# Out product, norms and turning in one block, the root's split last, and six edits to the attention, SSM and HGRN stages

## The reference, cut to what matters

```python
def first_block(x, ...):
    h = rms_norm(x, attn_pre_norm)
    h = dilated_attention_mixer(h, w_in, w_out, rel_bias)    # (o * silu(z)) @ w_out
    x = x + rms_norm(h, attn_post_norm)
    h = rms_norm(x, ssm_pre_norm)
    h = s5_mixer(h, ...)                                     # (y * silu(z)) @ w_out
    x = x + rms_norm(h, ssm_post_norm)
    return x

def s5_scan(u, a_re, a_im, log_dt, b, c, d_skip):            # 64 groups of 16 channels, 64 states
    a_bar = jnp.exp(A * dt)
    b_bar = ((a_bar - 1.0) / A)[..., None] * Bm
    states = associative_scan(combine, (a_bar, u @ b_bar))
    y = real(states @ C) + d_skip * u

def hgrn2(h, ...):                                           # 8 heads
    f = lb + (1.0 - lb) * sigmoid(f); logf = log(f); kin = 1.0 - f
    G = cumsum(logf); o = (q * exp(G)) @ state + tril(q, k, decay) @ v
    o = rms_norm_2(o, gnorm) * silu(g); return o @ w_out
```

## Time and profile before

| | us |
|---|---|
| median of 3 runs | 4160.52 |
| lowest, highest | 4149.19, 4170.95 |
| the profiled execution, its time | 4150.93 |
| its span | 4149.1 |
| TensorE busy | 3700.0 (89%) |
| VectorE busy | 1690.6 (41%) |
| ScalarE busy | 894.7 (22%) |
| GpSimd busy | 1896.0 (46%) |

### The profile page before, as it was taken

The page is one execution under the profiler, slowest core; times in us unless marked ns, Lnnn a source line. Parts: engine busy times, 40 slices in busy tenths (PEclk is TensorE's granted clock), DMA queues, the critical chain, the costliest instruction groups (busy, mean ns, idle before and its releaser), DMA issues. The chain is left out here.

```text
span 4149.1 us, 47884 instructions
## 1 busy us (share of the span) xinstructions
PE 3700.0 (89%) x18444; PEld 3021.7 (73%) x18444; DVE 1690.6 (41%) x2738; ACT 894.7 (22%) x2343; POOL 1896.0 (46%) x731
## 2 busy tenths in 40 slices
PE   8998987399788799999966899997899999879999
PEld 6777864278676588877855788875788877768887
DVE  2323137877536531132367411245521144652213
ACT  2333241111213410011033111013211112331111
POOL 5444431221343255655634465652356554335564
PEclk9999996687799799999988999998999999989999
DMA  3327851033222122222200222221222222212222
GB/s 135 103 92 93 109 79 42 25 92 92 67 88 73 68 83 97 96 92 90 97 21 1 77 102 101 91 102 51 77 92 92 101 85 90 72 69 89 101 91 81
DMA packets 95957, 342.06 MB, mean 82 GB/s; under 512 B 27078, under 2 KB 45766, under 8 KB 61208
## 3 DMA queue, kind: packets, MB, share of 16 engines
q1 hardware_dynamic: 83408, 314.22, 25.4%
q10 hardware_dynamic: 12360, 25.18, 1.8%
HBM read 318.39 MB, written 16.78 MB: 81 GB/s over the span
## 5 line engine op out<-in xcount | busy, mean ns | idle before, releaser
L294 POOL CAST wh<-raw 128x2048 fp32r<-128x2048 f32 x269 | 513.7, 1910 | 1778.3 <-PE bank L336 1424.2
L296 POOL TENSOR_TENSOR wl<-raw,wh 128x2048 fp32r<-128x2048 f32 x269 | 1243.6, 4623 | 21.5
L334 PE MATMUL bank<-XTh,wh 128*128 128x512 f32 (+1 forms) x2448 | 953.1, 389 | 45.0 <-DVE XTl L1028 15.0
L335 PE MATMUL bank<-XTh,wl 128*128 128x512 f32 (+1 forms) x2448 | 937.2, 383 | 0.0
L336 PE MATMUL bank<-XTl,wh 128*128 128x512 f32 (+1 forms) x2448 | 936.4, 383 | 0.0
L334 PEld LDWEIGHTS bank<-XTh,wh 128*128 128x128 f32 x2448 | 468.7, 191 | 155.4 <-issue 42.5
L336 PEld LDWEIGHTS bank<-XTl,wh 128*128 128x128 f32 x2448 | 467.4, 191 | 90.3
L335 PEld LDWEIGHTS bank<-XTh,wl 128*128 128x128 f32 x2448 | 469.0, 192 | 84.7
L334 PE MATMUL bank<-wh,XTh 128*128 128x512 f32 (+2 forms) x1056 | 393.0, 372 | 36.8 <-DVE XTl L1028 12.6
L335 PE MATMUL bank<-wh,HTl 128*128 128x512 f32 x1024 | 403.4, 394 | 0.0
L334 PE MATMUL bank<-wh,HTh 128*128 128x512 f32 x1024 | 401.7, 392 | 0.0
(11 more groups left out here) (343 smaller groups left out, 4233.7 us busy)
## 6 DMA issues: line engine op xcount, KB each, us to landing
raw<-in_weights SPq DMA_DIRECT2D x270, 1024.0 KB, 4.8
B<-bias_d ACTq DMA_DIRECT2D x8, 1024.0 KB, 5.6
B<-bias_a ACTq DMA_DIRECT2D x8, 512.0 KB, 10.7
bias_d<-O SPq DMA_DIRECT2D x16, 256.0 KB, 18.8
MO<-HS SPq DMA_DIRECT2D x64, 64.0 KB, 2.6
bc<-in_ln_g ACTq DMA_DIRECT2D x8, 512.0 KB, 6.7
bc<-in_ln_b ACTq DMA_DIRECT2D x8, 512.0 KB, 7.1
X<-in_x SPq DMA_DIRECT2D x4, 512.0 KB, 9.0
```

Source lines behind the costliest of these rows:

```text
L294: pool.tensor_copy(wh[s][:, :], raw[r][:, :]).then_inc(w_high.h, 1)
L296: pool.tensor_tensor(wl[s][:, :], raw[r][:, :], wh[s][:, :].bitcast(F32), ALU.subtract).then_inc(w_split.h, 1)
L334: nc.tensor.matmul(psum, sh, mh, start=first, stop=False)
L335: nc.tensor.matmul(psum, sl, mh, start=False, stop=False)
```

## The change

1. `out_phase` is one block, with the norms and the turning in it. VectorE no longer copies the banks: `weigh` multiplies them by the norm's vector into `Y`, and ScalarE squares out of PSUM. The roots, the addition, the second norm (where there is one, its gain is now a row vector and no longer applied after the turning) and the turning go token tile by token tile. Half 1 of the product is done in the order `LATE`. GpSimd splits three of the four weight chunks ahead of the first root and the last, the next stage's first, behind the last root.
2. The table of phases leaves `arithmetic`. It is now `phases`, called in `ssm_scan` on VectorE behind `add_skip(0)`, ahead of `prepare(1)`; a squaring takes 4 instructions instead of 6, and there are 8. The three pole tables have a semaphore of their own. SP waits for `phases` before one of its transfers, since the scratch `T` lies in memory that the transfer writes.
3. `outputs` interleaves the two groups of a pair.
4. The passes of the dilated attention are written out on TensorE.
5. In the sliding attention the projection comes behind `scores(j+3)`.
6. HGRN: the logarithms and scans stand before the token tiles (`G` lies in `Y`, which makes room); in `hgrn_heads` `W` has eight slots, squares have a buffer of their own and come at n = 3, and the root at n = 6.

```diff
-def out_phase(vec, transposed, scalars=None):
+tail = {k: signal("tail_" + k) for k in ("vectors", "sums", "root", "x_new", "x_sums", "x_root", "normed", "turned", "high", "low")}
+LATE = ((0, 0), (1, 0), (2, 0), (0, 1), (3, 0), (1, 1), (2, 1), (3, 1))
+def out_phase(vec, gain=None, scalars=None):
...
-        out_product(bc, [vec], squares, scalars)
-        norm_phase("rms_add", bc=bc, transposed=transposed)
-def out_product(bc, vecs, squares, scalars):
...
+        def split(first, n):
+            a = c0 + AHEAD + first
+            stream(pool, a, a + n, 2, lambda k, j: split_chunk(pool, k, j % RAW, j % SPLIT))
...
+        def root(tt):
+            r = st[:, tt:tt + 1]
+            pool.wait_ge(*at("sums", TT + tt + 1))
+            link(p.tensor_tensor(r, SQ[:, 0, tt:tt + 1], SQ[:, 1, tt:tt + 1], ALU.add))
+            link(p.tensor_scalar(r, r, 1.0, RMS_EPS, ALU.mult, ALU.add))
+            power(r, tail["root"])
...
+        split(0, 3)
+        root(0)
+        root(1)
+        x_root(0)
+        root(2)
+        x_root(1)
+        root(3)
+        x_root(2)
+        x_root(3)
+        split(3, 1)
+        link.done()
...
+        def turn(tt):
+            pe.wait_ge(*at("normed" if second else "x_new", tt + 1))
+            for half in range(2):
+                for k in range(4):
+                    r = nc.tensor.transpose(bank(half, tt)[:, P * k:P * k + P],
+                                            src[:, tt, 512 * half + P * k:512 * half + P * k + P], ident[:, :])
+                r.then_inc(tail["turned"].h, 1)
+        for kh in range(2):
+            for tt in range(TT):
+                out_tile(0, tt, kh)
+        for tt, kh in LATE:
+            out_tile(1, tt, kh)
...
+        def square(half, tt):
+            if tt == TT - 1:
+                act.wait_ge(w_used.h, CREDIT + c0 + 2 * half + 2)
+            else:
+                act.wait_ge(tile_done.h, pe_done + 3 * half + tt + 1)
+            a.activation(N[:, tt, cols(half)], bank(half, tt), ACT.Square, scale=D ** -0.5,
+                         accum_out=SQ[:, half, tt:tt + 1]).then_inc(tail["sums"].h, 1)
+        def x_square(tt):
+            if second:
+                act.wait_ge(*at("x_new", tt + 1))
+                a.activation(N[:, tt, :], X[:, tt, :], ACT.Square, scale=D ** -0.5,
+                             accum_out=st[:, TT + tt:TT + tt + 1]).then_inc(tail["x_sums"].h, 1)
...
+            square(0, tt)
+        square(1, 0)
+        square(1, 1)
+        x_square(0)
+        square(1, 2)
+        x_square(1)
+        square(1, 3)
+        x_square(2)
+        if not second:
+            high(0)
+        x_square(3)
+        for tt in range(second ^ 1, TT):
+            high(tt)
...
+        def weigh(half, tt):
+            dve.wait_ge(*at("sums", TT * half + tt + 1))
+            link(v.tensor_tensor(Y[:, tt, cols(half)], bank(half, tt), bc[0][:, cols(half)], ALU.mult))
+        def add(tt):
+            dve.wait_ge(*at("root", tt + 1))
+            v.scalar_tensor_tensor(X[:, tt, :], Y[:, tt, :], st[:, tt:tt + 1], X[:, tt, :], ALU.mult, ALU.add).then_inc(tail["x_new"].h, 1)
+        def norm(tt):
+            if second:
+                dve.wait_ge(*at("x_root", tt + 1))
+                v.scalar_tensor_tensor(N[:, tt, :], X[:, tt, :], st[:, TT + tt:TT + tt + 1], bc[1][:, :],
+                                       ALU.mult, ALU.mult).then_inc(tail["normed"].h, 1)
+        def low(tt):
+            for half in range(2):
+                dve.wait_ge(*at("high", 2 * tt + half + 1))
+                v.tensor_tensor(tokens(XTl, half, tt), blocks(bank(half, tt)), tokens(XTh, half, tt).bitcast(F32),
+                                ALU.subtract).then_inc(tail["low"].h, 1)
+        for tt in range(TT):
+            weigh(0, tt)
+        weigh(1, 0)
+        add(0)
+        weigh(1, 1)
+        add(1)
+        norm(0)
+        weigh(1, 2)
+        add(2)
+        norm(1)
+        weigh(1, 3)
+        add(3)
+        low(0)
+        norm(2)
+        low(1)
+        norm(3)
+        low(2)
+        low(3)
...
-            with pe.Fori(0, PASSES - 1) as i:
-                one_pass(i, False)
-            one_pass(PASSES - 1, True)
+            for i in range(PASSES):
+                one_pass(i, i == PASSES - 1)
...
         def fill(j, d):
-            if d == 0 and tile_at(j) is not None:
+            if d == (j >= 0) and tile_at(j) is not None:
                 project(tile_at(j))
...
     with ExitStack() as c:
-        G = sb("G", [P, TT, D], F32, c)
+        G = Y
         with ExitStack() as c2:
...
                     a.activation(SG[:, n % 2, :], PS[n % 4][:, :], ACT.Sigmoid).then_inc(a_b.h, 1)
+                for h in range(8):
+                    act.wait_ge(tile_free.h, tile_free.base + 9 + h)
+                    a.activation(LF[:, h, :], LF[:, h, :], ACT.Ln).then_inc(a_b.h, 1)
                 for n in range(8, 16):
                     wait_g(act, n)
                     a.activation(G[:, n % 4, 512 * (n // 4 - 2):512 * (n // 4 - 1)], PS[4 + n % 4][:, :], ACT.Sigmoid).then_inc(a_b.h, 1)
-                act.wait_ge(tile2_free.h, tile2_free.base + 16)
-                for h in range(8):
-                    a.activation(LF[:, h, :], LF[:, h, :], ACT.Ln).then_inc(a_b.h, 1)
...
                         v.tensor_scalar(KIN[:, h, :], LF[:, h, :], -1.0, 1.0, ALU.mult, ALU.add).then_inc(tile_free.h, 1)
+                for h in range(8):
+                    dve.wait_ge(a_b.h, a_b.base + 18 + h)
+                    v.tensor_tensor_scan(LF[:, h, :], ones[:, :], LF[:, h, :], 0.0, ALU.mult, ALU.add)
...
-                for h in range(8):
-                    dve.wait_ge(a_b.h, a_b.base + 26 + h)
-                    v.tensor_tensor_scan(LF[:, h, :], ones[:, :], LF[:, h, :], 0.0, ALU.mult, ALU.add)
...
+    SLOTS = 8
-        W = sb("W", [P, 4, S], F32, c)
+        W = sb("W", [P, SLOTS, S], F32, c)
+        squared = sb("squared", [P, 2, S], F32, c)
...
-        def w(b, n):
-            return W[:, (SL * b + n) % 4, :]
+        def w(h, n):
+            return W[:, (SL * h + n) % SLOTS, :]
...
-                    if n == 5 and 2 * i + b:
+                    if n == 6 and 2 * i + b:
...
+            if h >= 2:
+                act.wait_ge(head["sums"].h, head["sums"].base + 4 * (h - 1))
-                a.activation(Y[:, cc, P * h:P * h + P], PS[6 + b][:, P * cc:P * cc + P], ACT.Square,
+                a.activation(squared[:, b, P * cc:P * cc + P], PS[6 + b][:, P * cc:P * cc + P], ACT.Square,
...
-            sp.dma_start(d, t[x]).then_inc(sm["params"].h, 16)
+            sp.dma_start(d, t[x]).then_inc(sm["poles" if x in ("ssm_a_re", "ssm_a_im", "ssm_log_dt") else "params"].h, 16)
+        act.wait_ge(sm["poles"].h, 16 * 3)
...
+        dve.wait_ge(sm["params"].h, 16 * 6)
...
+    def phases(self, dve, link):
+        v, T, E = nc.vector, self.T, self.tab.E
+        mul, cmul = complex_ops(dve, link)
+        s = lambda k: self.s[:, k, :]
-        t2 = (s(14), s(15))
+        t1, t2 = s(14), s(15)
+        def square(o, x):
+            mul(t1, x[0], x[0])
+            mul(t2, x[1], x[1])
+            link(v.tensor_tensor(o[0], t1, t2, ALU.subtract))
+            link(v.scalar_tensor_tensor(o[1], x[0], 2.0, x[1], ALU.mult, ALU.mult))
-            cmul(nxt, cur, cur, *t2)
+            square(nxt, cur)
...
+            sp.wait_ge(*at("phases", 1))
...
-        for g in range(2 * QP):
-            lo, pr = 64 * (g % 2), g // 2
-            o = PS[6 + g % 2][:, 256 * (k % 2) + 64 * pr:256 * (k % 2) + 64 * pr + 64]
-            nc.tensor.matmul(o, MO[:, k % 2, pr, g % 2, :], U[:, 8 * k + g, :], start=True, stop=False)
+        place = lambda pr, g: PS[6 + g][:, 256 * (k % 2) + 64 * pr:256 * (k % 2) + 64 * pr + 64]
+        for pr in range(QP):
+            for g in range(2):
+                nc.tensor.matmul(place(pr, g), MO[:, k % 2, pr, g, :], U[:, 8 * k + 2 * pr + g, :], start=True, stop=False)
-                r = nc.tensor.matmul(o, CA[lo:lo + 64, k % 3, x, pr, 1:9, :].rearrange("p n c -> p (n c)"),
-                                     SPR[lo:lo + 64, x, pr, :], start=False, stop=x == 1)
+                for g in range(2):
+                    lo = 64 * g
+                    r = nc.tensor.matmul(place(pr, g), CA[lo:lo + 64, k % 3, x, pr, 1:9, :].rearrange("p n c -> p (n c)"),
+                                         SPR[lo:lo + 64, x, pr, :], start=False, stop=x == 1)
...
+        if not k:
+            scalars.phases(dve, link)
+            dve.sem_inc(sm["phases"].h, 1)
...
-    with ExitStack() as c:
-        out_phase(t["attn_post_norm"][0], False, SsmScalars(ssm_tables, c))
-    ssm_mixer(ssm_tables)
-out_phase(t["ssm_post_norm"][0], "layer0" in STAGES)
+    ssm_scalars = SsmScalars(ssm_tables, s_scope)
+    out_phase(t["attn_post_norm"][0], t["ssm_pre_norm"][0], ssm_scalars)
+    ssm_mixer(ssm_tables, ssm_scalars)
+out_phase(t["ssm_post_norm"][0])
```

(3 more changed lines are left out.)

150 lines of the change are left out of this document (89 added, 61 removed).

## The result

| | before | after |
|---|---|---|
| median of 4 runs, us | 4154.85 | 4037.57 |
| lowest, highest | 4148.5, 4170.95 | 4028.74, 4051.03 |
| profiled execution | 4150.93 | 4051.03 |
| its span | 4149.1 | 4049.2 |

The ratio is 0.9715, 95% interval 0.9674 to 0.9756: 101 to 135 us less. Forecast were 4063 and a range of 4029 to 4098. The two profiled executions differ by 99.9 us, where the prediction's sum had 92.6. The profiled execution of after is the slowest of its four.

The account below looks back on a forecast made before the run. TensorE, busy 89% of 4149.1 us, was taken as the bound: only its idle or repeated time can be won. Terms sum to -92.6, from 4150.9 to 4058.3; half of 9.6 added gives 4063, range 4029 to 4098.

Parts of the forecast that it names:

- Written-out passes: Dilated attention: TensorE's two gaps at the loop's returns, 2.91 and 11.02 us, both vanish, -13.9 us.
- First tail: Norms between the first two layers: 70.8 us from last product to next shrink to 20.5, -50.3 us.
- The table: Table of phases moved into the SSM scan: all of it on the path, with shorter squarings, +27.2 us.
- Outputs in pairs: SSM scan's outputs: CA products of two groups overlap in row halves, -11 us, bounds -4 and -25.
- Second tail: The stretch from T = 1165.3 to 1185.16: 19.8 us shrink to 10.4, -9.4 us (-4 to -12).
- Heads: HGRN's heads: eight slots let ScalarE run ahead; a quarter of VectorE's 31.9 us wait goes, -8 us.
- Sliding attention: Projection behind the scores: three quarters of TensorE's 22.6 us of waits for probabilities go, -17 us.
- (d): Rival: written-out passes in dilated attention stall on instruction fetches, slower, up to 4220 us; chance 0.03.
- (a): Rival: some overlaps in outputs, heads and sliding attention do not come, 22 us less gain, 4085; chance 0.2.
- (b): Rival: more is hidden: outputs -20, heads -20, tail 16 instead of 20.5, so 4037 us; chance 0.12.
- (c): Rival: the gaps of TensorE's loop stay, 13.9 us less gain, 4077 us; chance 0.07.
- (e): Rival: no change that can be told, 70 us of terms failing together; chance 0.03.

Follow-up runs that it names:

- the inverse edit: The loop of TensorE's passes in the dilated attention put back into the changed kernel: median 4066.58 us of 4 runs.

## Why the prediction was right

The measured 4037.57 lies in the range, 25.4 below the forecast. The profiled executions' difference of 99.9 was 7.3 more than the sum of 92.6. The prediction then added 4.7 because the median before lay above its profiled execution. After, the median lies 13.5 below its profiled one, so this term had the wrong sign; 7.3, 4.7 and 13.5 are the 25.4. Of the mechanism all but the heads held. Point by point:

- **Written-out passes, -13.9: mis-sized, -17.2.** The gaps were right; the low clock behind each of them, 1.6 and 1.9 us, was left out, though a stretch just behind them would have shown it.
- **First tail, -50.3: -50.8.** The queue of low parts behind `high(0)` was there, and so was the split's hold. That the sum came within 0.5 is in part luck: the hold was 3.9 for the 2.5 charged, `norm(2)` stood in the queue as well, and the low parts of tile 2, which were charged, came behind the last norm, beside its turning.
- **The table, +27.2: +27.1.** All of it was on the path, nothing of it was hidden, and the eight squarings were sized right. That it would have cost as much in the old place, so that moving it gains nothing, was not said.
- **Outputs in pairs, -11: about -14.7.** The last two outputs gave 10.2, of which the gate's longer low clock took back 1.6: 8.6 for the 8.5 forecast. (The 10.2 already has in it 1.2 lost to the new wait for `MO`.) The steady steps gave 6.1 for 2.5, and their term was mis-sized twice over: a step's outputs save 4.9 of TensorE, not 2.4, and they save nothing where VectorE is held but all of it in the step without a split.
- **Second tail, -9.4: -9.4.** The split held the last addition, 2.82 instead of 1.28, 1.5 for the 1.0 charged.
- **Scans, -10.2: -9.0**, and 8.9 when undone. TensorE's wait itself fell by exactly the 10.2, from 14.68 to 4.48.
- **Heads, -8: -5.7, and the reason was wrong.** The step that failed is "Eight slots let ScalarE run ahead": four slots are as fast. The cause of the gain stays open.
- **Sliding attention, -17: -19.6.** More of the waits went than three quarters of 22.6.
- **The working.** Three numbers of it don't come out and change nothing in the sum. The product's last three tiles end 2.7 us apart and not 4.7, since a record of 0.39 starts 0.23 behind the one before it. All of the outputs on the path would be 8.5 + 14.4 = 23 and not 25. And rival (d) would decide from eight stalls on (78.7 / 11.02), while the range by its own working is 4026 to 4096.
- **Rivals.** (a) fell with the outputs and the sliding attention. (b) is the nearest: its 4037 is the median that came, but not by its parts; the tail was not 16, the heads gave no 20, and the outputs gave 14.7 of its 20. (c), that the gaps stay, is refuted by the inverse edit; the 0.3 us that a branch and a compare-and-branch of the Trainium skill ("Advanced Engine Details and Errata", Control Flow Timing) would give is not what a return costs here, 2.88 and 10.36. (d), slower by fetching in a row, is refuted: 131 packets, and no stall that the loop hadn't. That sequential code hides its fetches and a far branch doesn't, as the Trainium skill has it ("Runtime: NRT & Kernel Launch", Instruction fetch mechanics), these runs agree with. (e), no change that can be told, fell with the measured 101 to 135.

## What to carry to other kernels

A stage that moves work from one wait to another shows a large gain in the place where it was and the same loss in the place where it is; add both before calling it a gain, as with the 27 us of the table. Where two engines wait for each other in turn by equal amounts in every step, look for an order that only the program text imposes; taking `prepare` a step ahead gave 33 us of the scan. Where work is taken off an engine and a wait of the same length appears, as TensorE's 4.8 did behind the paired outputs, a second chain is as long, and the gain comes only when that one is shortened too. And a wait that changes its name without changing its length, as VectorE's 31 us in the heads, is a sign of the same.

## What the runs showed of the hardware

- A return of TensorE's loop of some 1560 instructions stalled it for 2.9 us where the DMA share in the gap was 0.13 to 0.14, and for 10.4 to 11.0 where it was 0.89 to 0.90. With the low clock behind it the first cost 4.6 us and the second 12.7 to 13.0.
- GpSimd's work on SBUF held VectorE's fp32 instructions whose operands all lay in SBUF until GpSimd's instruction was over: 1.28 us became 2.11, 4.34 and 5.63, two products of 128x512 became 7.20 from 1.42, and an instruction on 128x32 took 4.37 instead of 0.19. Instructions with one operand in PSUM kept their time beside the same split. It goes the other way too: GpSimd's instruction on 128x1 took 1.13 instead of 0.19 while a norm of 1.29 ran on VectorE (718.62 in the first tail after).
- Products on the two halves of the array's rows overlapped fully when they alternated: `CA` of two groups took 1.12 us at the low clock, `CA` of one group 1.11 before. At the high clock it was 0.66 for two, and 0.66 for one before.
